# Work at the seams of a four-layer network put in another order, and one pair's bias sums ahead of a softmax's maximum

## The reference

```python
def first_block(x, ...):                     # layer 0: mixer A, layer 1: mixer B
    for layer in range(2):
        hn = rms_norm(h, attn_norm[layer])
        h = h + (swa_sink_mixer(hn) if layer == 0 else nsa_mixer(hn))
        h = h + swiglu(rms_norm(h, ffn_norm[layer]))
    return rms_norm(h, final_norm)
# A: 16 heads, 2 key heads, window 128, bias by distance, sinks in the softmax
# B: o = g0 * compressed attention (31 blocks; keys through gelu(flat @ w1) @ w2, w1 of 2048 x 256)
#      + g1 * selected attention (16 best of 8 blocks of 64, so all) + g2 * window 512
def second_block(x, c, positions, ...):      # layer 0: mixer E, layer 1: mixer O
    for l in range(2):
        shift, scale, gate = split(silu(c) @ ada_w[l] + ada_b[l], 3)
        h = x * (1 + scale) + shift
        y = even_mixer(h) if l == 0 else mla_mixer(h, positions)
        x = layer_norm(DEEPNORM_ALPHA * x + (1 + gate) * y)
# E: u, v, z_a, x_b, z_b = split(h @ w_in); a = u * (W_s LN(v) + b) * silu(z_a)
#    b = multiscale_pool(x_b) * silu(z_b); concat(a, b) @ w_out
# O: latent attention with rope (angles = positions * inv), gated by silu(z), @ w_out
```

## Time and profile before

| what | value |
|---|---|
| median of 3 runs | 1974.44 us |
| profiled execution | 1973.71 us, span 1972.0 us |
| TensorE (PE) busy | 1928.4 us, 98% of the span, 9826 matmuls |
| VectorE (DVE) busy | 1051.9 us, 53% |
| ScalarE (ACT) busy | 828.3 us, 42% |
| GpSimd (POOL) busy | 793.2 us, 40% |
| DMA | 209.52 MB in all |
| chain of work that ended last | PE 87%, DVE 5%, issue 2%, ACT 1%, POOL 1% |

### The profile page before, as it was taken

One profiled execution on the slowest core, in us unless ns is written; L12 is line 12 of the kernel. 1 busy time (PEld: TensorE's weight loads), 2 busy tenths in 40 slices (PEclk: granted clock), 3 DMA queues, 4 the chain that ended last, 5 costly groups with the idle time before them and its releaser, 6 DMA issues.

```text
span 1972.0 us, 29532 instructions
## 1 busy us (share of the span) xinstructions
PE 1928.4 (98%) x9826; PEld 1624.1 (82%) x9826; DVE 1051.9 (53%) x2323; ACT 828.3 (42%) x1527; POOL 793.2 (40%) x392
## 2 busy tenths in 40 slices
PE   7999999999999999999999999999999999999997
PEld 5898888888878899888888888888788888888886
DVE  5564655321274777546653445666614565666645
ACT  4564322222353777543222323422223356666622
POOL 3633544444354211145444443444544332424441
PEclk9999999999999999999999999999999999999999
DMA  7532555322234112125453332333232221212221
GB/s 239 179 107 96 192 171 180 106 96 96 96 108 141 39 48 79 38 96 202 161 185 107 101 96 86 97 98 105 94 102 97 65 86 54 78 55 80 65 85 43
DMA packets 70020, 209.52 MB, mean 106 GB/s; under 512 B 9739, under 2 KB 15115, under 8 KB 69948
## 3 DMA queue, kind: packets, MB, share of 16 engines
q1 hardware_dynamic: 57724, 174.72, 27.3%
q10 hardware_dynamic: 12224, 33.85, 5.3%
HBM read 196.90 MB, written 8.49 MB: 104 GB/s over the span
## 4 chain that ended last, share of the span: by engine, by line
PE 87%; DVE 5%; issue 2%; ACT 1%; POOL 1%; DVEq 0%; ACTq 0%; POOLq 0%
PE bank L1025 22%; PE bank L1027 22%; PE bank L1026 22%; PE bank L1393 3%; PE bank L1571 2%; PE bank L1590 2%; PE bank L1342 2%; PE bank L1373 1%; PE bank L1445 1%; PE bank L1243 1%; PE bank L1582 1%; PE bank L1450 1%; PE bank L1389 1%; PE bank L1231 1%; POOL wsp L471 1%
## 5 line engine op out<-in xcount | busy, mean ns | idle before, releaser
L471 POOL TENSOR_TENSOR wsp<-raw,wsp 128x1024 fp32r<-128x1024 f32 (+2 forms) x291 | 706.2, 2432 | 933.4 <-ACT wsp L581 930.0
L1025 PE MATMUL bank<-xs,wsp 128*128 128x512 f32 x1304 | 514.7, 395 | 4.7 <-DVE mid L2199 1.7
L581 ACT ACTIVATE wsp<-raw 128x1024 fp32r<-128x1024 f32 (+2 forms) x294 | 302.7, 1037 | 508.7 <-PE bank L1027 465.6
L1027 PE MATMUL bank<-xs,wsp 128*128 128x512 f32 x1304 | 508.9, 390 | 0.0
L1026 PE MATMUL bank<-xs,wsp 128*128 128x512 f32 x1304 | 508.6, 390 | 0.0
L1025 PEld LDWEIGHTS bank<-xs,wsp 128*128 128x128 f32 x1304 | 245.4, 188 | 57.5 <-issue 7.7
L1027 PEld LDWEIGHTS bank<-xs,wsp 128*128 128x128 f32 x1304 | 245.2, 188 | 51.6
L1026 PEld LDWEIGHTS bank<-xs,wsp 128*128 128x128 f32 x1304 | 245.6, 188 | 50.0 <-issue 1.0
L1025 PE MATMUL bank<-gsp,wsp 128*128 128x512 f32 x512 | 200.4, 391 | 1.6 <-issue 1.2
L1027 PE MATMUL bank<-gsp,wsp 128*128 128x512 f32 x512 | 199.6, 390 | 0.0
L1026 PE MATMUL bank<-gsp,wsp 128*128 128x512 f32 x512 | 199.4, 389 | 0.0
(11 more groups left out here) (321 smaller groups left out, 2761.6 us busy)
## 6 DMA issues: line engine op xcount, KB each, us to landing
raw<-weights SPq DMA_DIRECT2D x294, 512.0 KB, 3.5
gen<-ada ACTq DMA_DIRECT2D x48, 512.0 KB, 3.5
tmp<-mid SPq DMA_DIRECT2D x64, 128.0 KB, 2.9
bias_b<-bias_row ACTq DMA_DIRECT2D x1, 4096.0 KB, 37.5
mid<-bias_b SPq DMA_DIRECT2D x8, 512.0 KB, 4.0
hT<-xT SPq DMA_DIRECT2D x2, 1024.0 KB, 9.5
bias_a<-bias_row ACTq DMA_DIRECT2D x1, 2048.0 KB, 17.6
mid<-bias_a SPq DMA_DIRECT2D x8, 256.0 KB, 2.8
```

Source lines behind the costliest of these rows:

```text
L471: pool.tensor_tensor(wsp[:, slot, 1, 0:w], raw[:, slot, 0:w], wsp[:, slot, 0, 0:w].bitcast(F32), ALU.subtract).then_inc(w_ready, 1)
L581: act.activation(wsp[:, u % RING, 0, 0:w], raw[:, u % RING, 0:w], ACT.Copy).then_inc(hi_done, 1)
L1025: pe.matmul(dst, w[0], x[0], start=first, stop=False)
L1027: return pe.matmul(dst, w[1], x[0], start=False, stop=last)
```

## The change

It changes orders, and gives a few steps to another engine, at nine places:

- Start: the bias rows' matmuls go to banks 3 to 6; ScalarE squares first, then copies the bias rows and stores them, and splits unit `A_K + 3` ahead of the norm's square root and `A_V + 3` behind it. The first square of every RMS norm but the final one goes to PSUM bank 7, and DVE's running sum lives there, so that one of its two operands is in PSUM.
- Start of A: the remainders of the first pair's queries go from GpSimd to DVE, with its sinks copy, ahead of the last query's scaling.
- End of A and of B: the first input of the output projection is made one (A) or two (B) slots sooner, and the loop's last turn-out runs inside `project_out`, between its first units' matmuls.
- Norm 2: its mean matmul goes from behind tile 4 of unit `B_KS` to behind tile 1.
- Compression weights: DVE's units are `B_W1 + 2`, `B_W1 + 4` and `B_Q` instead of `B_W1 + 4`, `B_W1 + 6` and `B_Q`.
- Gelu: its transposes go inside the first query projection, after 5 of its 8 tiles, and at its beginning.
- Start of B: the second bias sums (`b_bias(1, 0)`) go from behind the subtraction of the maximum in the last compressed softmax to ahead of its maximum; `keep_running` goes, and TensorE computes score 3 ahead of `c_turn`, then a transpose and values; scores wait for each half of the queries on its own.
- B loop: DVE copies out (`b_keep`) ahead of the slot's outputs (`b_outputs`) instead of behind them.
- E: the first u unit is multiplied ahead of the last pooling group's mix; the angles go into the inputs of E's output projection, behind tiles 4, 6 and 9.

```diff
@@ -60,7 +60,7 @@
-SHARED = (B_W1 + 4, B_W1 + 6, B_Q)
+SHARED = (B_W1 + 2, B_W1 + 4, B_Q)
@@ -499,14 +499,17 @@
+                    if not i:
+                        pool.wait_ge(qs_ready, 2)
...
-            for n in range(PAIRS):
+            pool.wait_ge(qs_hi, 2)
+            for n in range(1, PAIRS):
                 pair_queries(n % 2, n // 2)
-            split_units(A_O + AHEAD, B_W1 + 4)
-            for u in range(B_W1 + 4, B_Q + RING):
+            split_units(A_O + AHEAD, B_W1 + 2)
+            for u in range(B_W1 + 2, B_Q + RING):
@@ -589,7 +592,7 @@
-            def squares(n, held=()):
+            def squares(n, held=(), between=None):
@@ -602,7 +605,11 @@
+                    if n < NORM_FINAL and j == 0:
+                        dst = bank[7][:, :]
                     act.activation(dst, hT[:, j, :], ACT.Square).then_inc(sq_ready, 1)
+                if between is not None:
+                    between()
@@ -680,20 +687,23 @@
-            act.wait_ge(brow_mm, 4)
-            for n in range(4):
-                w = BIAS_COLS // 4
-                act.activation(brow[:, w * n:w * n + w], bank[1 + n][0:HEADS, 0:w], ACT.Copy).then_inc(brow_copied, 1)
-            act.wait_ge(brow_copied, 4)
-            act.dma_start(bias_row, brow).then_inc(bias_stored, 16)
-            squares(0)
+
+            def bias_rows():
+
+                act.wait_ge(brow_mm, 4)
+                for n in range(4):
+                    w = BIAS_COLS // 4
+                    act.activation(brow[:, w * n:w * n + w], bank[3 + n][0:HEADS, 0:w], ACT.Copy).then_inc(brow_copied, 1)
+                act.wait_ge(brow_copied, 4)
+                act.dma_start(bias_row, brow).then_inc(bias_stored, 16)
+
+            squares(0, (A_K + AHEAD,), bias_rows)
+            split_hi(A_V + AHEAD)
...
-            split_hi(A_K + AHEAD)
-            split_hi(A_V + AHEAD)
@@ -745,13 +755,13 @@
-            for u in range(8, 11):
+            for u in range(8, 12):
...
-                for u in range(11 + 4 * v, 15 + 3 * v):
+                for u in range(12 + 3 * v, 15 + 3 * v):
@@ -884,7 +894,7 @@
-            first_input(MID_E, True, E_U)
+            first_input(MID_E, True, E_U + 1)
@@ -1189,13 +1199,13 @@
-                pe.matmul(bank[1 + n][0:HEADS, 0:w], gen[0:33, 0:HEADS], gen[0:33, 16 + w * n:16 + w * n + w],
+                pe.matmul(bank[3 + n][0:HEADS, 0:w], gen[0:33, 0:HEADS], gen[0:33, 16 + w * n:16 + w * n + w],
...
-            pe.wait_ge(brow_copied, 4)
...
+            pe.wait_ge(brow_copied, 4)
@@ -1260,17 +1270,19 @@
-                run_slot(((a_scores, 0), (a_transpose, 2), (a_values, 3), (a_turn_out, 4)), 8, s, i, last)
+                stages = ((a_scores, 0), (a_transpose, 2), (a_values, 3), (a_turn_out, 4))
+                run_slot(stages[:3] if last and s == 8 + 3 else stages, 8, s, i, last)
...
-            project_out(A_O, DC, XK_A, [0, 1, 2, 3, 4, 5, 6], mid_ready, MID_A + DC)
+            project_out(A_O, DC, XK_A, [0, 1, 2, 3, 4, 5, 6], mid_ready, MID_A + DC,
+                        between=lambda: a_turn_out(8 - 1, PAIRS // 2 - 1))
...
-            project(B_KS, bank[2][:, :], part=range(5))
+            project(B_KS, bank[2][:, :], part=range(2))
             mean_square(2)
-            project(B_KS, bank[2][:, :], part=range(5, DC))
+            project(B_KS, bank[2][:, :], part=range(2, DC))
@@ -1292,15 +1304,15 @@
-            pe.wait_ge(q_free, 9)
-            pe.wait_ge(gelu_ready, 1)
-            project(B_Q, bank[0][:, :])
...
+                if v == 0:
+                    pe.wait_ge(q_free, 9)
+                project(B_Q, bank[0][:, :], part=range(5, DC) if v else range(5))
@@ -1333,8 +1345,8 @@
-                if m % 8 == 0:
-                    pe.wait_ge(qs_ready, i * 4 + (2 * DC + 2 * pp + 2))
+                if m % 8 < 2:
+                    pe.wait_ge(qs_ready, i * 4 + (2 * DC + 2 * pp + e + 1))
@@ -1408,16 +1420,20 @@
-                    pe.wait_ge(b_s_ready, 4)
-                    keep_running(bank[2], 6)
+                    b_scores(3, 0)
...
+                    b_transpose(1, 0)
+                    b_values(0, 0)
+                    return
...
-                run_slot(((b_transpose, 2), (b_scores, 0), (b_values, 3), (b_turn_out, 4)), 16, s, i, last)
+                stages = ((b_transpose, 2), (b_scores, 0), (b_values, 3), (b_turn_out, 4))
+                run_slot(stages[:3] if last and s == 16 + 3 else stages, 16, s, i, last)
...
-            project_out(B_O, DC, XK_B, [0, 1, 2, 3, 4, 5, 6], mid_ready, MID_B + DC)
+            project_out(B_O, DC, XK_B, [0, 1, 2, 3, 4, 5, 6], mid_ready, MID_B + DC,
+                        between=lambda: b_turn_out(16 - 1, PAIRS // 2 - 1))
@@ -1488,15 +1504,22 @@
-            pool_mix(3, E_U - 1)
...
-            with pe.Fori(0, DC // 2) as i:
+
+            def gated(p, i):
+                pe.wait_ge(u_out, i * 2 + (p + 1))
+                project(E_U + 2 * p, bank[2 * p][:, :], i)
+                if isinstance(i, int) and p == 0:
+                    pool_mix(3, E_U - 1)
+                pe.wait_ge(za_silu, i * 2 + (p + 1))
+                project(E_U + 2 * p + 1, bank[2 * p + 1][:, :], i)
+
+            gated(0, 0)
+            gated(1, 0)
+            with pe.Fori(1, DC // 2) as i:
                 for p in range(2):
-                    pe.wait_ge(u_out, i * 2 + (p + 1))
-                    project(E_U + 2 * p, bank[2 * p][:, :], i)
-                    pe.wait_ge(za_silu, i * 2 + (p + 1))
-                    project(E_U + 2 * p + 1, bank[2 * p + 1][:, :], i)
+                    gated(p, i)
@@ -1666,6 +1689,10 @@
+                if n < NORM_FINAL:
+                    dve.tensor_tensor(rstd[:, :] if j == DC - 1 else bank[7][:, :], tmp[:, j % 4, :], bank[7][:, :],
+                                      ALU.add).then_inc(sq_used, 1)
+                    return
@@ -1700,13 +1727,19 @@
-            def out_inputs(n, xk_base, deep=False):
+            def out_inputs(n, xk_base, deep=False, between=None):
...
+                if between is not None:
+                    for k in range(1, n):
+                        rest(k)
+                        if k in between:
+                            between[k]()
+                    return
@@ -1812,12 +1845,23 @@
+            def sinks_of(pp, i):
+
+                dve.tensor_copy(tb[pp][:, :, SINK:SINK + 1],
+                                row("sinks", HEADS)[:, bass.ds(i * 2 + 8 * pp, 2)].unsqueeze(2)).then_inc(a_sink, 1)
+
...
+                if c == DC - 1:
+                    for e in range(2):
+                        dve.wait_ge(qs_hi, e + 1)
+                        dve.tensor_tensor(qs[0][e][1], q_raw[0][e], qs[0][e][0].bitcast(F32), ALU.subtract
+                                          ).then_inc(qs_ready, 1)
+                    sinks_of(0, 0)
@@ -1833,8 +1877,8 @@
-                    dve.tensor_copy(tb[pp][:, :, SINK:SINK + 1],
-                                    row("sinks", HEADS)[:, bass.ds(i * 2 + 8 * pp, 2)].unsqueeze(2)).then_inc(a_sink, 1)
+                    if m or not isinstance(i, int) or i:
+                        sinks_of(pp, i)
@@ -1871,7 +1915,7 @@
-                if last and s == 8 + 3:
+                if last and s == 8 + 2:
@@ -1921,11 +1965,13 @@
+            split_lo(SHARED[0])
...
-            split_lo(SHARED[0])
+            split_lo(SHARED[1])
             def b_query(k, i):
-                dve.wait_ge(q_ready, i * RING + (DC + k + 1 - RING))
+                if i:
+                    dve.wait_ge(q_ready, i * RING + (DC + k + 1 - RING))
@@ -1940,13 +1986,12 @@
-            for u in SHARED[1:]:
-                split_lo(u)
-            b_query(0, 0)
+            split_lo(SHARED[2])
...
+            b_query(0, 0)
@@ -1970,14 +2015,14 @@
+                if between is not None:
+                    between()
...
-                if between is not None:
-                    between()
@@ -2050,9 +2095,12 @@
-                if last and s == 16 + 3:
+                if last and s == 16 + 1:
+                    b_norm(16 - 1, i)
                     first_input(XK_B)
-                run_slot(((b_norm, 2), (b_bias, 0), (b_outputs, 3), (b_keep, 4)), 16, s, i, last)
+                    b_outputs(16 - 2, i)
+                    return
+                run_slot(((b_norm, 2), (b_bias, 0), (b_keep, 4), (b_outputs, 3)), 16, s, i, last)
@@ -2172,15 +2220,19 @@
-            pool_out(3, E_U)
+            pool_out(3, E_U + 1)
...
-            dve.wait_ge(pos_in, 16)
-            step(dve.tensor_copy(turns, posi))
-            step(dve.tensor_scalar(ang, turns, col("inv"), None, ALU.mult))
-            for n, (shift, dst) in enumerate(((0.0, arg), (0.25, turns))):
-                work = dst
+            def angles():
+
+                dve.wait_ge(pos_in, 16)
+                step(dve.tensor_copy(turns, posi))
+                step(dve.tensor_scalar(ang, turns, col("inv"), None, ALU.mult))
+
+            def reduced(n):
+
```

(4 more changed lines are left out.)

## The result

The changed kernel takes 1957.64 us (median of 6 runs, 1955.0 to 1959.2), the kernel before 1975.58 (6 runs): a ratio of 0.991, interval 0.9897 to 0.9922, 17.9 us less. The profiled execution after took 1957.34 us around a span of 1955.5, that is 16.4 less than the one before (1973.71).

A forecast was written before the change was run, and what follows sets the result against it. TensorE was taken as the bound, busy 1928.4 of 1972.0 us, so only its waits and slow clock could be regained. Terms summing to 18.6 off 1973.71 gave 1955.1, plus 0.73 for the median 1955.8 us; range 1950.5 to 1963.

The forecast's parts named there:

- Start: Kernel start: squares first and unit 3's half earlier remove TensorE waits of 1.89 and 1.25; gain 3.1 us.
- A's start: Start of attention A: first pair's query remainders move to DVE, taking 0.6 us off the 1.53 wait for the last statistics.
- Rival 2: Start of attention A: the bias_b transfer sets A's start; 1959.5 us, at worst 1961.2; chance 0.10.
- End of A, gelu: A's turn-out and first-input waits go, gain 0.6 us; the wait behind the transposed gelu's copy goes, gain 0.7.
- End of B: B's output projection: the waits ahead go and its half-clock stretch runs at full speed; gain 3.1 us.
- Norm 2: Mean matmul moved up three tiles in unit B_KS: 0 us, bounds -2 and 0.
- Compression weights: Compression stage: DVE's earlier units put GpSimd's chain one step (2.43) sooner; gain 2.1 us, bounds 0.5 and 2.75.
- Start of B: Last compressed softmax: bias sums ahead of the maximum lengthen the path; cost 0.4 us, bounds gain 0.9 and loss 2.
- fourth rival: From B's start: without keep_running the clock falls to 0.50 and stays through the loop, adding 52.5 us, 2008; chance 0.04.
- B loop: Attention B's loop: copying out ahead of the outputs removes 5.9 us of waits; gain 6.0, bounds 1 and 7.5.
- Rival 1: B loop: the wait only moves, 5 of the 6.0 us return on a score or output; 1960.8 us; chance 0.12.
- Mixer E: Mixer E: waits for the pooled input (1.15) and behind the angle steps (1.66) go; gain 2.8 us.

The follow-up runs named there:

- e9_sums_sbuf: The changed kernel with the running sums of the norms wholly in SBUF again: 1961.4 us.
- e7_lo_pool: The changed kernel with the remainders of the first pair's queries on GpSimd again, the sinks copy staying ahead: 1957.31 us.
- e12_before_title: The kernel before, with only the second bias sums moved ahead of the maximum in the last compressed softmax: 1975.29 us.
- e1_fill: The changed kernel with the six calls of keep_running put back at the start of attention B, ahead of score 3: 1955.65 us.
- e8_fill_shared5: The changed kernel with keep_running put back at B's start and the remainders of units B_W1+6 and +7 on DVE as well: 1955.36 us.
- e2_before_nofill: The kernel before, with only keep_running at the start of attention B and the wait ahead of it removed: 1977.2 us.
- e4_shared5: The changed kernel with the remainders of compression units B_W1+6 and +7 on DVE as well: 1957.59 us.

## Why the prediction was right, point by point

The forecast was 1955.8 and the time is 1957.64, inside the range. The traces differ by 16.5 where the sum had 18.6; the B loop, B's start and the compression weights fall short by 5.3 together, and the other terms give 3.2 more than forecast. Part of the match is luck: the pair of traces has the start's best case and, in the kernel before, a half clock at B's end that another trace of the same order hasn't.

- **What bounds the kernel**: right. TensorE's busy time is the same, and the span fell by its waits.
- **Start** (3.1 forecast, 3.75 in this pair, 2.4 to 3.8 over the traces): right in size. The step that the sums follow the squares "step for step" hid an edit: they follow without delay because they lie in PSUM (e9_sums_sbuf).
- **A's start** (0.6 forecast, 1.6): undersized, and for the wrong reason. The prediction credited the remainders' move to DVE; e7_lo_pool gives that 0.25 at most. What went from the path is the sinks copy on DVE (1.23 us), to which the sum gave no term. The bound that it set by bias_b wasn't at work: the landing moved by as much as TensorE did, and a later one cost nothing. Rival 2 didn't come.
- **End of A, gelu** (0.6, 0.7 forecast; 1.0, 0.8): right.
- **End of B** (3.1 forecast, 3.3): right against this trace. The 1.4 for the waits measure 1.8; the 1.7 for the half clock are 1.6, but the old order doesn't always lose them: the same waits leave the clock at 1.00 in e12_before_title.
- **Norm 2** (0): right by the sums' place. The Trainium skill ("SBUF — State Buffer", section "Who interferes with whom") says that a DVE instruction with at most one SBUF input, outside the two-port modes, doesn't contend with GpSimd. Here the longest of 24 such sums took 697 ns, and with both operands in SBUF 2717: the trace agrees. What the prediction weighed this rule for, the two query remainders, ran in 0.69 and 0.68 us, without a long form. It was worth 3.6 us of the norms' stretches and 3.8 in the median, where the prediction had put 0 for norm 2, with -2 as its bound, and no term for the sums' place at the start.
- **Compression weights** (2.1 forecast, 0.76): the term that was mis-sized. The step that failed is that the chain on GpSimd would be "one step (2.43) sooner by the units that TensorE waits for". It is sooner up to the sixth unit; the last two became GpSimd's own, one behind the other, with 1.57 and 0.73 of waits, of which 1.17 is GpSimd's own wait for a late load, a thing that the term didn't hold. "At most one such" wait was a sign of being right, and there are two. The prediction's bound of 0.5 covers it.
- **Start of B** (-0.4 forecast, -2.2): the path's 0.4 measures 0.05 (e1_fill) to 0.3 (e12_before_title). The clock, which the prediction kept as its fourth rival at 52 us, did fall, but for 6.83 us and not through the loop, and cost 2.0 (e1_fill). The step that failed is the sentence that set the rival's price: it had the loop's short matmuls unable to bring the clock back, and they ran at 1.00 again from 651.49 on. As a term of the sum it would have been a loss of 2; the bound of 2 that stands there names another cause.
- **B loop** (6.0 forecast, 3.8): the copy's order was right and its size was off by 2.2. Rival 1 came with 2.2 of its 5: what is seen of it are waits of the transposes' weight loads in the same slots, 1.7 in sum and at most 0.3 each, too short to appear among TensorE's own waits.
- **Mixer E** (2.8 forecast, 3.5): right, and the angles' cover held. That its two edits can't be had one by one was not seen.
- **The title's edit**: costed at 0.4 lost, measured at 0.3 of path or less and nothing in the time.

## What to carry to other kernels

A table of when the bound engine starts the same instruction in two traces says seam by seam what each edit gave, where the list of waits only says what is left; use it before choosing experiments, and make it for every trace that leaves a stretch unchanged, since one pair can show as a gain what only that execution had. Edits at one seam aren't additive: undoing one of two can cost several times what both gave, so price them together and say what each hides for the other. Before removing work without a use from an engine that then waits, look at the granted clock behind that wait, and price a fall by the same instructions at either level: at B's start it cost 0.9 to 2.6 us here, not the loop's 52.

## What was not expected of the hardware

The granted clock fell and rose in stretches of 3.41, 6.83 or 10.24 us, and with the same waits to a hundredth it fell in one kernel (e8_fill_shared5) and not in another (e1_fill). Nor did the longer wait bring the longer fall: e2_before_nofill had 0.50 for 3.42 behind 2.13, the changed kernel 6.83 behind 1.95, and e4_shared5 3.41 behind 1.96. At B's end 1.06 and 0.34 brought a fall in the kernel before and none in e12_before_title. The Trainium skill ("TensorE: Matmul & The Clock Gate", section "What's actually happening") says that the gate's watch runs freely and isn't reset by a kernel's start; that would let equal waits end differently, and no run here separates it from other causes.

A sum on DVE of two 128x512 operands in SBUF took up to 2956 ns in a trace (e12_before_title), against 693 in the median, and with one operand in PSUM at most 697 in every trace that has it. A copy of 128x2 numbers took 0.15 us with GpSimd idle and 1.23 with its subtraction beside it, both ending at 77.3.
